# A product-key expert mixer: from gathering each token's experts to passing the whole table over blocks of tokens

## The reference, cut to what matters

```python
def peer(xn, w_query, sub_keys, expert_u, expert_v):   # per block of tokens
    q = (xt @ w_query).reshape(blk, 8, 2, 128)
    s = jnp.einsum('thcd,cnd->thcn', q, sub_keys)
    s1, i1 = lax.top_k(s[:, :, 0], 16)
    s2, i2 = lax.top_k(s[:, :, 1], 16)
    cand = s1[..., :, None] + s2[..., None, :]          # 256 sums a head
    sc, pos = lax.top_k(cand, 16)
    idx = ...                                           # i1 * 128 + i2 at pos
    g = jax.nn.softmax(sc)
    act = gelu(einsum('thkd,td->thk', expert_u[idx], xt))
    return einsum('thk,thkd->td', g * act, expert_v[idx])

h = h + mix @ w_out;  m = rmsnorm(h, g_ffn);  h = h + peer(m, ...)
h = h + (p_l @ w_ple) * sigmoid(rmsnorm(h, g_ple) @ w_ple_gate);  y = rmsnorm(h, g_final)
```

## Time and profile before

| | us |
|---|---|
| median of 2 runs (3959.33 and 3964.27) | 3961.8 |
| the profiled execution | 3962.55 |
| its span, first to last instruction | 3960.8 |
| from the start to the first instruction of `experts` | 844.8 |
| `experts`, to the first instruction of `finish` | 2879.7 |
| `finish`, to the end of the span | 236.3 |

### The profile page before, as it was taken

One profiled execution on the slowest core, in us unless ns is written; L12 is line 12 of the kernel. 1 busy time (PEld: TensorE's weight loads), 2 busy tenths in 40 slices (PEclk: granted clock), 3 DMA queues, 4 the chain that ended last, 5 costly groups with the idle time before them and its releaser, 6 DMA issues. The chain is left out here.

```text
span 3960.8 us, 33923 instructions
## 1 busy us (share of the span) xinstructions
PE 2314.9 (58%) x9722; PEld 797.2 (20%) x9722; DVE 2290.5 (58%) x5501; ACT 1128.1 (28%) x3649; POOL 1274.0 (32%) x1247
## 2 busy tenths in 40 slices
PE   7999826965564563464456456346445645534587
PEld 3555413433110110020011011002001101100133
DVE  4235134627487568558658756855965874685322
ACT  3222104411223223322322322332232232222233
POOL 0000021300444344344434434434443443444100
PEclk9899957988675675675567567568556756755799
DMA  2201137960999999999999999999999999999711
GB/s 98 87 28 54 35 128 251 348 236 14 399 417 421 400 410 421 421 385 421 422 395 422 422 405 412 421 421 394 421 421 395 422 421 391 409 421 421 272 54 46
DMA packets 216893, 1265.70 MB, mean 320 GB/s; under 512 B 27493, under 2 KB 30394, under 8 KB 81330
## 3 DMA queue, kind: packets, MB, share of 16 engines
q0 software_dynamic: 165008, 1147.82, 70.5%
q1 hardware_dynamic: 44410, 98.60, 7.3%
q10 hardware_dynamic: 7296, 17.21, 1.2%
HBM read 1241.58 MB, written 26.47 MB: 320 GB/s over the span
## 5 line engine op out<-in xcount | busy, mean ns | idle before, releaser
L2232 DVE CUSTOM_DVE_ANT_0 ex_ring<-ex_ring,ex_rows 128x1024 f32<-128x1024 f32 x1056 | 1290.9, 1223 | 877.1 <-DMA ex_ring<-in_expert_uv,ex_idx_cur 865.8
L2149 POOL DMA_INDIRECT ex_ring<-in_expert_uv,ex_idx_cur x1056 | 1164.0, 1102 | 1691.3 <-PE ex_acc L2271 1375.9
L2271 PE MATMUL ex_acc<-ex_ring,ex_diag 128*32 128x512 f32 x4224 | 888.5, 914 | 1192.2 <-ACT ex_diag L2187 1161.0
L2178 ACT ACTIVATE ex_act_out<-ex_dots 128x2 f32<-128x2 f32 x528 | 107.2, 203 | 1783.9 <-DVE ex_dots L2232 1783.6
L2271 PEld LDWEIGHTS ex_acc<-ex_ring,ex_diag 128*32 128x32 f32 x4224 | 108.7, 130 | 1919.0 <-ACT ex_diag L2187 1757.7
L1880 PE MATMUL ex_pk<-ex_w,ex_aT 128*128 128x512 f32 x576 | 280.7, 631 | 57.2 <-DVE ex_aT L1928 57.2
L2187 ACT ACTIVATE ex_diag<-ex_pick_row,ex_coef 128x32 f32<-128x32 f32 x1056 | 282.2, 314 | 49.3 <-ACT ex_coef L2181 0.8
L2181 ACT ACTIVATE ex_coef<-ex_act_out,ex_gate_cur 128x1 f32<-128x1 f32 x1056 | 253.3, 287 | 17.4
L293 PE MATMUL pj_bank<-pj_aT,pj_wbuf 128*128 128x512 f32 x512 | 224.7, 594 | 0.4 <-ACT pj_aT L408 0.4
L1861 PE MATMUL ex_pt<-ex_wo,ex_aT 128*128 128x512 f32 x288 | 153.5, 684 | 46.3 <-DVE ex_aT L1928 38.8
L2409 PE MATMUL fi_pg<-fi_wg,fi_aT 128*128 128x512 f32 x288 | 140.7, 646 | 32.5 <-PEq L76 32.5
(11 more groups left out here) (352 smaller groups left out, 2476.7 us busy)
## 6 DMA issues: line engine op xcount, KB each, us to landing
ex_ring<-in_expert_uv,ex_idx_cur POOLq DMA_INDIRECT x1056
at_ring<-in_cache_kT POOLq DMA_DIRECT2D x64, 256.0 KB, 6.3
at_ring<-in_cache_kT SPq DMA_DIRECT2D x64, 256.0 KB, 8.0
at_ring<-in_cache_v SPq DMA_DIRECT2D x64, 256.0 KB, 7.8
at_ring<-in_cache_v POOLq DMA_DIRECT2D x64, 256.0 KB, 6.3
pj_wbuf<-in_w_in SPq DMA_DIRECT2D x6, 2048.0 KB, 9.2
ex_ring<-in_w_queryT ACTq DMA_DIRECT2D x4, 2048.0 KB, 23.3
fi_x<-mid_h SPq DMA_DIRECT2D x10, 512.0 KB, 3.6
```

The source lines that it names most:

```text
L2149: pool.indirect_dma_start(ring[:, c % RING, :], None, t["expert_uv"], bass.IndirectOffsetOnAxis(idx_cur[k % 2][:, i:i + 1], 0)).then_inc(c ...
L2178: act.activation(act_out[:, half, :], dots[:, half, :], ACT.Gelu).then_inc(gelu_done, 1)
L2232: dve.tensor_tensor_reduce(out=u, in0=u, in1=rows[:, j, :], scale=1.0, scalar=0.0, op0=ALU.mult, op1=ALU.add, accum_out=dots[:, q % HALVES ...
L2271: mm = pe.matmul(acc[n][quarter(j), :], diag[:, q % HALVES, p, :], ring[:, c % RING, D + n * 512:D + (n + 1) * 512], start=False, stop=las ...
```

## The change

`experts` and `finish` go, and `route` and `dense` take their place. `route` makes the output projection, the norm, and the scores of all 9 tiles, one tile behind another, stores them, and searches tiles 0 and 1. `dense` reads the whole table, in 128 blocks of 128 experts, once for each of four passes over 256 tokens (the last pass has 288, with the 32 sample tokens). The u half of the table is laid out transposed, so that a block of it is 8 stationary operands of 128x128.

For a block, `hidden` makes gelu's argument for 128 experts x 256 tokens in 8 matmuls, `bend` the gelu on ScalarE, `weigh` multiplies it on VectorE by a dense gate matrix (zero where a token doesn't use an expert), and `values` adds 128 tokens x 1024 in two halves for two tiles, 4 matmuls of 512 columns. The dense gate matrix of a token is 128x128 and is made as a product over the token's 128 slots of two one-hot matrices, one of them scaled by the gates; it goes through DRAM. Tiles 0 and 1 get theirs before the first pass; the others, the searches (on VectorE, two steps of the generator behind each block) and the end of the layer of earlier tiles run beside the blocks. The ends of the last two tiles and of the sample tokens come behind the last pass.

```diff
-    experts(nc, t)
-    finish(nc, t)
+    with ExitStack() as ctx:
+        fd = Finder(Stage(nc, ctx, "fd"))
+        route(nc, t, fd)
+        dense(nc, t, fd)
...
+# route, TensorE
+                turn(pe, "x0")
+                project_out(pe, 0)
+                turn(pe, "x1")
+                project_out(pe, 1)
+                turn(pe, "m0")
+                fold(pe)
+                turn(pe, "m1")
+                score(pe, 0)
+                turn(pe, "x2")
+                score(pe, 1)
+                project_out(pe, 2)
+                for f in range(2, TILES):
+                    if f + 1 < TILES:
+                        turn(pe, f"x{f + 1}")
+                        project_out(pe, f + 1)
+                    turn(pe, f"m{f}")
+                    score(pe, f)
...
+# dense: RING = 5, AHEAD = 4, SPAN = 8, CH = 16, LOT = 4, PERIOD = 36
+        def load_block(sp, i):
+            if i >= RING:
+                sp.wait_ge(v_done, i - RING + 1)
+            b = i % NB
+            sp.dma_start(ring[:, i % RING, :], t["expert_uv"][b * P:(b + 1) * P, :]).then_inc(came[i % RING], 16)
...
+        def hidden(pe, i):
...
+            for c in range(KT):
+                mm = pe.matmul(ps[i % 2][:, 0:T[p]], ring[:, i % RING, c * P:(c + 1) * P], mT[p % 2][:, c, 0:T[p]],
+                               start=(c == 0), stop=(c == KT - 1))
+            mm.then_inc(s_done, 1)
+
+        def values(pe, i):
+            p, b = divmod(i, NB)
+            pe.wait_ge(weighed, i + 1)
...
+            for j in range(2):
+                for n in range(2):
+                    mm = pe.matmul(y[2 * j + n][:], hid[:, i % AHEAD, j * P:(j + 1) * P],
+                                   ring[:, i % RING, D + n * 512:D + (n + 1) * 512], start=(b == 0), stop=(b == NB - 1))
+            if p + 1 == PASSES:
...
+                for n in range(2):
+                    mm = pe.matmul(few[n * DEC:(n + 1) * DEC, :], hid[:, i % AHEAD, 2 * P:2 * P + DEC],
+                                   ring[:, i % RING, D + n * 512:D + (n + 1) * 512], start=(b == 0), stop=(b == NB - 1),
+                                   tile_position=(0, n * DEC))
+            mm.then_inc(v_done, 1)
+
+        def bend(act, i):
...
+            act.activation(hid[:, i % AHEAD, 0:T[p]], ps[i % 2][:, 0:T[p]], ACT.Gelu).then_inc(gelu_done, 1)
+
+        def weigh(dve, i):
...
+            dve.tensor_tensor(part, part, gin[gi % 2][:, 0:T[p] // CH, i % SPAN, :], ALU.mult).then_inc(weighed, 1)
...
+        def gates_tensor(pe, f):        # a lot is 4 tokens: 32 lots a tile, 8 for the sample tokens
...
+            for u in range(lots(f)):
+                k = lot(f, u)
+                pe.wait_ge(l_up, k + 1)
+                pe.wait_ge(r_up, k + 1)
+                pe.wait_ge(lot_out, k)
...
+                for q in range(LOT):
+                    mm = pe.matmul(lot_bank[:, q, :], picks[:, 0, k % 2, q, :], picks[:, 1, k % 2, q, :], start=True, stop=True)
+                mm.then_inc(lot_done, 1)
+                yield
...
+        # gates_scalar, for a lot
+                act.wait_ge(lot_done, k + 1)
+                act.activation(staged[:, ch % 2, :, at:at + LOT].rearrange("p i q -> p q i"), lot_bank, ACT.Copy).then_inc(
+                    lot_out, 1)
+        # gates_vector, four for a lot
+                    ins = dve.tensor_scalar(picks[:, 0, k % 2, q, :], fd.iota[:], slots[f % 2][:, 1, tok:tok + 1],
+                                            slots[f % 2][:, 2, tok:tok + 1], ALU.is_equal, ALU.mult)
+        # gates_pool, four for a lot
+                        ins = pool.tensor_scalar(picks[:, 1, k % 2, q, :], fd.iota[:], slots[f % 2][:, 0, tok:tok + 1], None,
+                                                 ALU.is_equal)
...
+        # end_tensor, for a tile: 8 transposes, then for each half 8 gate matmuls and 2 of the per-layer input
+                for c in range(KT):
+                    mm = pe.matmul(bank[0:n, :], kit.aT[:, c, 0:n], wg[:, c, half * 512:(half + 1) * 512],
+                                   start=(c == 0), stop=(c == KT - 1))
...
+            @block.tensor
+            def _(pe):
+                for f in range(2):
+                    for _ in gates_tensor(pe, f):
+                        pass
+                hidden(pe, 0)
+                for p in range(PASSES):
+                    sides = [gates_run(gates_tensor, pe, p), ends_run(end_tensor, pe, p, end_bank)]
+                    for b in range(NB):
+                        i = p * NB + b
+                        if i + 1 < BLOCKS:
+                            hidden(pe, i + 1)
+                        values(pe, i)
...
+                        for side in sides:
+                            next(side, None)
...
+                last_ends(end_tensor, pe, BANKS)
```

More of the change, by code:

```diff
@@ new lines, in add_rest, with norm @@
+        def add_rest(dve, f):
+            n = size(f)
+            for half in range(2):
+                dve.wait_ge(projected, 2 * f + half + 1)
+                part = xx[f % 2][0:n, half * 512:(half + 1) * 512]
+                dve.tensor_tensor(part, part, pj[half][0:n, :], ALU.add).then_inc(h1_ready, 1)
+        def norm(dve, f):
+            n = size(f)
+            dve.wait_ge(rooted, f + 1)
+            dve.reciprocal(rs[f % 2][0:n], rs[f % 2][0:n]).then_inc(inverted, 1)
+            dve.wait_ge(inverted, f + 1)
+            dve.scalar_tensor_tensor(out=mx[f % 2][0:n], in0=xx[f % 2][0:n], scalar=rs[f % 2][0:n], in1=g[0:n],
+                                     op0=ALU.mult, op1=ALU.mult).then_inc(m_ready, 1)
@@ new lines, in _, with seek, some @@
+                take_v(dve, "m1")
+                def seek():
+                    for f in range(2):
+                        dve.wait_ge(copied, 4 * (f + 1))
+                        yield from fd.search(dve, v, f, scores(f))
+                        fd.lower(dve, v, f).then_inc(negated, 1)
+                steps = seek()
+                def some(n):
+                    for _ in range(n):
+                        next(steps, None)
+                take_v(dve, "x2")
+                some(22)
@@ new lines, in _ @@
+                add_rest(dve, 2)
+                take_v(dve, "x3")
+                some(4)
+                norm(dve, 2)
+                some(4)
+                add_rest(dve, 3)
+                take_v(dve, "m2")
+                some(4)
+                norm(dve, 3)
+                for f in range(4, TILES):
+                    some(9)
+                    take_v(dve, f"x{f}")
+                    some(7)
+                    add_rest(dve, f)
+                    take_v(dve, f"m{f - 1}")
+                    some(4)
+                    norm(dve, f)
@@ new lines, in gates_run, with end_pool @@
+        def gates_run(part, eng, p):
+            yield from pause(PERIOD)
+            for f in next_tiles(p):
+                yield from part(eng, f)
+        def end_pool(pool, j, kit, use):
+            n = size(j)
+            if use:
+                pool.wait_ge(kit.x_up, use)
+                pool.wait_ge(kit.added, 2 * use)
+            pool.dma_start(kit.h1[0:n, :], t["h1"][j * P:j * P + n, :]).then_inc(kit.h_in, 16)
+            pool.dma_start(kit.pT[:, :, 0:n], t["pT"][j * P:(j + 1) * P, :].rearrange("p (k q) -> p k q", q=P)[:, :, 0:n]).then_inc(
+                kit.p_in, 16)
+            yield from pause(16)
+            pool.wait_ge(kit.y_up, use + 1)
+            pool.dma_start(t["y"][j * P:j * P + n, :], kit.out[0:n, :]).then_inc(kit.stored, 16)
@@ new lines, in ends_run, with last_ends @@
+        def ends_run(part, eng, p, *bank):
+            if p == 0:
+                return
+            yield from pause(2)
+            for j in (2 * p - 2, 2 * p - 1):
+                before = 0
+                for _ in part(eng, j, kits[0], j, *bank):
+                    before += 1
+                    yield
+                yield from pause(17 - before)
+        def last_ends(part, eng, banks):
+            runs = [part(eng, PT - 2 + k, kits[k], PT - 2 if k == 0 else 0, *banks[k]) for k in range(3)]
+            while runs:
+                runs = [r for r in runs if next(r, eng) is not eng]
@@ new lines, in _ @@
+                for p in range(PASSES):
+                    sides = [find_vector(dve, v, p), gates_run(gates_vector, dve, p), ends_run(end_vector, dve, p, end_bank)]
+                    for b in range(NB):
+                        weigh(dve, p * NB + b)
+                        if b == 0 and p:
+                            sums_v(dve, p - 1)
+                        if b == 0 and p == 1:
+                            dve.wait_ge(ends_in, 32)
+                        for side in sides:
+                            next(side, None)
```

1174 lines of the change are left out of this document (600 added, 574 removed).

## The result

The changed kernel takes 5669.3 us (median of two runs, 5669.0 and 5669.7) where the kernel before takes 3961.8: 1.431 times as long, with a 95% interval from 1.428 to 1.434. The forecast was 5550 with a range of 5430 to 5815. The time is 119 us over the forecast, 2.1%.

A forecast was written before the change was run, and what follows sets the result against it. Gathered bytes bound the kernel before; TensorE's float32 columns would bound it after. 845 + 475 (`route`) + 183 (first lots, start, gates) + 3685 (blocks) + 289 (beside work) + 72 (behind) = 5549 us of span, forecast 5550, range 5430 to 5815.

The forecast's parts named there:

- The bound: Four passes: TensorE's float32 columns are the bound, 6.87 us a block in passes 1 to 3, blocks 3685 us; chance 0.82.
- a pass that differs from 880 us by more than a tenth: Sign of being wrong: a pass of 128 blocks that isn't within a tenth of 880 us.
- the beside work: TensorE's own work between the blocks: token lots of tiles 2 to 8 and ends of six tiles, adding fully, 289 us.
- the last pass's pair: Two matmuls of 32 weight columns a block for the sample tokens, side by side, 0.86 us, bounds 0.86 and 1.72.
- Rival A: Matmul streams run closer than the rows, 0.276 us or less per 512-column record, so the kernel isn't slower; chance 0.02.
- Rival B: In-order engine queues stall TensorE; 1 us in each block gives 6060 us; chance 0.11 for beyond 5800.
- Rival C: TensorE gets half the clock, 1.2 GHz, in the passes, giving 9520 us; chance 0.01.
- rival D: The kernel takes less than the sum of the terms, below 5430 us; chance 0.04.
- the lots ahead of the first pass: 64 lots making gate matrices of tiles 0 and 1, standing alone: 2.6 us each, 166 us, bounds 115 and 256.
- The last pass: Fourth pass over the table, `hidden` with 288 columns: 8.16 us a block, 1045 us for 128 blocks.
- `route`: Front stage of projections, scores and first searches, hidden by nothing: 475 us, bounds 445 and 540.
- Behind the last pass: Three interleaved ends 54 us, plus 18 for sums, first add, last norm and store: 72 us.

## Why the prediction was right, and where it was off

**The bound.** The forecast said that TensorE's columns take the place of the gathers' bytes and that two thirds of the span would be blocks at 6.87 us. Right: 6.89 us measured, TensorE busy 1000 us of 1000 at a clock of 1.00. The whole kernel's bytes came to 852 MB, where the forecast has some 820, and the DMA share in the passes to 0.48, with 0.51 to 0.52 in the first three and 0.40 in the last, where it has under 0.5. The bytes saved were of no use, and the run with more bytes shows it. One of the forecast's signs of being wrong was badly set: a pass that differs from 880 us by more than a tenth. The four passes take 939, 975, 983 and 1119 us, so three of them show the sign although the bound is the one forecast. The 880 leaves out the beside work and the last pass's pair, which the forecast's own sum has: by it three passes would be 976 on average and the last at least 1045.

**Rival A** (streams run closer) is out: a record of 512 columns took 3.43 / 8 = 0.429 us, against the 0.276 that it needed. The rule behind its 3815 us, the spacing of 131 ns from the Trainium skill (TensorE: Matmul & The Clock Gate, Back-to-back issue gap), doesn't hold here: a float32 matmul of 512 columns still takes 0.858 us, and by that rule it would be 0.524, as the forecast has it.

**Rival B** (stalls) is out: 5.7 us idle before 4096 records of `values`, and a period 1.73 us shorter still had no stall. One of its premises was partly right: GpSimd's one-hot took 0.60 us by itself (four in 2.42), above the 0.29 to 0.41 from the earlier trace rows. In the passes this is hidden; ahead of them it is not. **Rival C** is out by the clock of 1.00, **rival D** by every term being at or above the forecast.

**The beside work** in the passes was about right: a lot 0.89 for 0.90, and 283 us in all for the 289, taking 6.89 and 8.50 us a block off the four passes. The passes' excess of 42 us is, to within a few us, the last pass's.

**The step that was mis-sized most: the lots ahead of the first pass**, "I take 2.6, near the half-clock end". It was 3.27 us, 64 of them and a few turns between tiles 212 us for the 166, and the start and the first gates 19 for 17. The mechanism was the one named, TensorE and ScalarE taking turns at one bank. The value taken was below its own terms already: 1.97 + 0.58 + 0.15 is 2.70. TensorE's part was the half-clock value, 2.05 for 1.97. ScalarE's copy was 1.04 us where the earlier trace rows has 0.58 for 128x512 without gaps in the output; the allowance of up to 0.6 for its scattered writes was in the bounds, and the value taken left it out. 2.05 + 1.04 + 0.17 = 3.26. The two-bank run shows that the copy was in the period.

**The last pass**, "I take the pair as one matmul, 0.86": 1.17 us. That the two overlap is right (one after the other would be 1.72). What was left out is what comes with the change between 128 and 32 weight columns: 0.09 us before and 0.11 behind, which the run without the pair shows, and 0.12 within the pair, which stays unexplained. (8.49 - 8.16) x 128 = 42 us.

**`route`**, 491 for 475. Two rows of TensorE's timeline in the kernel after, a product with `w_out` and a tile's scores:

```profile
1053.53 13.97 PE L1937 MATMUL rt_pj<-rt_wo,rt_aT 128*128 128x512 f32 x32 [0.83 <-ACT rt_aT L1981]
...
1070.27 29.43 PE L1964 MATMUL rt_pk<-rt_w,rt_mT 128*128 128x512 f32 x64 [1.90 <-ACT rt_mT L1981]
```

Behind a wait of 0.83 us a product takes its 13.97. Behind one of 1.90 the scores take 29.43, 1.7 over the 27.70 of the earlier trace rows. Eight of the later products are longer by 1.7 to 2.2 us in this way, some 14 of the 16 us, in a stretch with a granted clock of 0.94. The forecast costed the waits of both handoffs but not the clock behind them. It isn't so every time: one score with the same wait, at 1024.09, took 27.73. Between executions of the same `route` it differs too. In the run with four column groups, four of the five scores behind a wait of 1.90 were short, like this one:

```profile
1076.28 27.73 PE L1964 MATMUL rt_pk<-rt_w,rt_mT 128*128 128x512 f32 x64 [1.90 <-ACT rt_mT L1981]
```

There `route`, from its first load to the first instruction of `dense`, took 481.1 us (853.76 to 1334.83), against 488.5 (847.35 to 1335.84) in the kernel after, and the shorter products make up the 7.4 us; the granted clock from 1050 to 1150 was 1.00 there and 0.97 in the kernel after. So about half of the excess of `route` is there in one execution and not in the next. Why the same wait is followed by either length stays open; no run took the waits away.

**Behind the last pass**, 83 for 72. The gate and per-layer products of the three ends keep TensorE busy from 5596.0 to 5649.1, 53 us, as forecast (54). What lies around them took 30 us for 18: 12 from the last block to the first gate product, with TensorE's transposes waiting twice for other engines, and 18 from the last product to the end of the span.

## What to carry to other kernels

Count matmul records before counting bytes: a dense form that reads fewer bytes loses if its multiplications, in float32, fill TensorE for longer than the gathers filled the DMA engines. Here 3685 us of columns stood against 3116 us of everything that they replaced, and the columns' price could be read from short streams in the old trace. When a wait's releaser in the profile is an instruction that the program doesn't need yet, look for another that ended just before it; here, a copy out of the only bank. And when two profiles are compared, measure the stretch that the edit changed: the untouched part ahead of the lots moved by up to 10 us from one execution to another.

## What the runs showed of the hardware that was not expected

- Changing between weights of 128 and of 32 columns cost about 0.1 us on each side: `values` 3.53 for 3.44, `hidden` 3.99 for 3.88. Whether the narrow matmuls took 0.98 or 0.57 us made no difference to it, and a lot with 128 columns of weights at the same place cost its neighbours nothing.
- TensorE's granted clock went with the gaps between the same short bursts of eight records: gaps of 1.2 us, a clock of 0.50 to 0.55 and 2.05 us a burst; gaps of 0.3 us, 0.94 and 1.16 us. The same 64 records behind the same wait of 1.90 us took 27.73 us or 29.43, in one execution and from one to another.
- A ScalarE copy of 128x512 from PSUM that writes each number 64 bytes behind the last took 1.04 us, against 0.578 for one without gaps. The Trainium skill (SBUF — State Buffer, Specifications (TRN2)) says that each crossing to a new line of 16 bytes pays a penalty; that fits, as every number here opens a line, but no run changed the layout alone.
- A comparison of 128x128 against a scalar for each partition took 0.60 us on GpSimd and 0.29 to 0.35 on VectorE.
- A float32r matmul has one record, and four of 512 columns took 1.02 to 1.05 us, 0.26 each: more than a quarter of float32's 0.858, which is 0.215. Why was not tried.
- Another megabyte copied within DRAM in each block, which took the DMA share to 0.82, lengthened the passes by nothing that shows (4015.7 us for 4016.5).
